# First piece behind two residual norms taken in five chunks as separate products on the residual and on the unscaled new term

## What is computed

```
x = x + rms_norm(mixed, mix_post_g)      # mixed = (gates ...) @ w_out
h = rms_norm(x, ffn_pre_g)
gt, up = split(h @ w_gate_up)            # 2 x 2816 columns
f = (silu(gt) * up) @ w_down
x = x + rms_norm(f, ffn_post_g)
h = rms_norm(x, norm1_g_2)               # second block
z = h @ w_in_2                           # lru_x first (1024 columns)
```

## Time and profile before

| what | value |
|---|---|
| median of three runs | 909.71 us |
| the profiled execution | 910.08 us, of which 908.0 us are the span of instructions |
| TensorE, VectorE, ScalarE, GpSimd busy | 99%, 81%, 64%, 4% of the span |
| granted TensorE clock | 0.999 in the mean, 9 (90% or more) in each of 40 slices |
| HBM traffic | 177 GB/s over the span |
| chain that ended last | TensorE 66%, issue 24%, VectorE 6%, ScalarE 2% |

### The profile page before, as it was taken

The page is one execution under the profiler, slowest core; times in us unless marked ns, Lnnn a source line. Parts: engine busy times, 40 slices in busy tenths (PEclk is TensorE's granted clock), DMA queues, the critical chain, the costliest instruction groups (busy, mean ns, idle before and its releaser), DMA issues.

```text
span 908.0 us, 18312 instructions
## 1 busy us (share of the span) xinstructions
PE 899.3 (99%) x6623; PEld 847.7 (93%) x6623; DVE 736.6 (81%) x1361; ACT 580.8 (64%) x998; POOL 38.0 (4%) x50
## 2 busy tenths in 40 slices
PE   9999999999999999999999999999999999999997
PEld 7999999999999999998888888999999999999886
DVE  5999898888989988689888646889979988888533
ACT  5649878797877575566666535679656755666332
POOL 1000111111110000000000000100000000000000
PEclk9999999999999999999999999999999999999999
DMA  9577588877875647456555555445447455555601
GB/s 335 181 267 231 143 199 236 248 219 218 241 203 192 209 166 247 145 161 236 196 186 185 193 187 170 147 171 189 143 134 257 158 192 185 182 179 175 228 1 47
DMA packets 48510, 172.04 MB, mean 189 GB/s; under 512 B 5668, under 2 KB 6344, under 8 KB 48328
## 3 DMA queue, kind: packets, MB, share of 16 engines
q1 hardware_dynamic: 43488, 154.74, 51.2%
q0 software_dynamic: 2880, 10.49, 6.1%
q10 hardware_dynamic: 2088, 6.08, 1.8%
HBM read 159.72 MB, written 1.09 MB: 177 GB/s over the span
## 4 chain that ended last, share of the span: by engine, by line
PE 66%; issue 24%; DVE 6%; ACT 2%; DMA 1%; POOL 1%; SPq 0%; POOLq 0%; ACTq 0%; DVEq 0%
PE A L472 10%; PE A L473 10%; PE A L474 10%; PE B L696 5%; PE A L504 4%; PE B L504 3%; PE B L472 2%; PE B L473 2%; PE B L474 2%; PE A L506 2%; DVE w_lo L1397 2%; PE B L506 2%; PE B L777 2%; PE A L777 1%; PE A L485 1%
## 5 line engine op out<-in xcount | busy, mean ns | idle before, releaser
L1397 DVE TENSOR_TENSOR w_lo<-raw,w_hi 128x1024 fp32r<-128x1024 f32 x249 | 301.8, 1220 | 72.7 <-ACT w_hi L930 72.1
L930 ACT ACTIVATE w_hi<-raw 128x1024 fp32r<-128x1024 f32 x249 | 259.4, 1051 | 74.6 <-PE A L778 20.9
L472 PE MATMUL A<-h,w_hi 128*128 128x256 f32 x952 | 274.5, 288 | 0.2 <-DVE sc L2017 0.2
L474 PE MATMUL A<-h,w_lo 128*128 128x256 f32 x952 | 269.2, 283 | 0.0
L473 PE MATMUL A<-h,w_hi 128*128 128x256 f32 x952 | 269.2, 283 | 0.0
L472 PEld LDWEIGHTS A<-h,w_hi 128*128 128x128 f32 x952 | 182.1, 191 | 3.3 <-issue 2.6
L473 PEld LDWEIGHTS A<-h,w_hi 128*128 128x128 f32 x952 | 182.3, 191 | 0.3
L474 PEld LDWEIGHTS A<-h,w_lo 128*128 128x128 f32 x952 | 182.2, 191 | 0.0
L472 PE MATMUL B<-h,w_hi 128*128 128x256 f32 x352 | 100.1, 284 | 0.0
L473 PE MATMUL B<-h,w_hi 128*128 128x256 f32 x352 | 99.6, 283 | 0.0
L474 PE MATMUL B<-h,w_lo 128*128 128x256 f32 x352 | 99.6, 283 | 0.0
(11 more groups left out here) (313 smaller groups left out, 1635.0 us busy)
## 6 DMA issues: line engine op xcount, KB each, us to landing
raw<-in_weights_dram SPq DMA_DIRECT2D x289, 512.0 KB, 4.3
w_lo<-raw POOLq DMA_DIRECT2D x20, 512.0 KB, 4.8
csrow<-cs_dram ACTq DMA_DIRECT2D x9, 512.0 KB, 4.9
x<-in_x_dram SPq DMA_DIRECT2D x4, 256.0 KB, 5.3
bd<-in_lru_w_dram ACTq DMA_DIRECT2D x1, 1024.0 KB, 5.7
out_dram<-m_wide SPq DMA_DIRECT2D x3, 256.0 KB, 2.1
raw<-in_weights_dram SPq DMA_DIRECT2D x2, 256.0 KB, 4.8
par<-in_params_dram SPq DMA_DIRECT2D x1, 379.0 KB, 6.3
```

The source lines that it names most:

```text
L472: mm(dst, wh, lo, start=first, stop=False, skip_group_check=free)
L474: return mm(dst, wl, hi, start=False, stop=last, skip_group_check=free)
L930: F(w_hi[:, s, :], raw[:, s, :], ACT.Copy).then_inc(hi_ready, 1)
L1397: V.tensor_tensor(w_lo[:, s, :], raw[:, s, :], w_hi[:, s, :].bitcast(F32), ALU.subtract).then_inc(lo_ready, 1)
```

## The change

For five chunks (1 to 5) of the first piece behind each norm the product of the weights with `g*(x + m*s*gm)` is taken in two parts: one on `g*x` with the old residual, and one on `g*gm*m` with the new term before its scale `s`. The second goes to a bank of its own, VectorE multiplies it by `s` and adds it to the output of the first piece. TensorE takes two chunks of the first part, then the sums, then three more chunks, the spread, and then the five chunks of the second part (`apart_residual`); the dummy products go, and in `scaled_four` the first piece leaves out these chunks. ScalarE makes ten high parts for each norm (`x_part`, `m_part`), VectorE ten low parts. For the first norm they are made between the pieces of the preceding stage. For the second norm, the parts on `x` are made by ScalarE at the beginning of the down projection and by VectorE between `split_rest_lo(0)` and `lru_rates`, the parts on `m` with the output chunks. VectorE copies the scale and multiplies the second product (`m_products_scaled`) between `residual_scaled` and `sum_squares`. The diff, with context cut:

```diff
@@ -82,6 +82,7 @@
 DOWN1_REST = KF - 2 * KD
+APART = (1, 2, 3, 4, 5)
@@ -184,10 +185,14 @@
         zero = sb("zero", [P, P], F32R)
+        gains = sb("gains", [P, 2, KD])
         mean = sb("mean", [P, T])
...
         scale = sb("scale", [P, TT])
+        s0a = ExitStack()
+        m_stage = sb("m_stage", [P, 2 * T], F32R, s0a)
+        s0a.close()
         stage = sb("stage", [P, 2, T])
@@ -235,6 +240,8 @@
+
+        m_apart = sb("m_apart", [P, len(APART) - 2, 2 * T], F32R, s4)
         s4.close()
@@ -313,6 +320,12 @@
+
+        mix_x = {k: hid[:, KD + k, :] for k in APART}
+        mix_m = {k: hid[:, 2 * KD + k, :] for k in APART}
+        down_x = {k: h[:, k, :] for k in APART}
+        down_m = {k: m_apart[:, i - 2, :] if i > 1 else m_stage[:, :] if i else hid[:, KF, :] for i, k in enumerate(APART)}
+        mix_apart, down_apart = B[:, 0, 0:T], B[:, 3, 0:T]
@@ -368,6 +381,9 @@
         last_scale = sem("last_scale")
+        gains_ready, x_high, x_low, m_high, m_low = (
+            sem("gains_ready"), sem("x_high"), sem("x_low"), sem("m_high"), sem("m_low"))
+        m_products, m_scaled, apart_added = sem("m_products"), sem("m_scaled"), sem("apart_added")
@@ -541,6 +557,21 @@
+            def apart_residual(p, n, bank, evacuated, summed_n, norm_n, squares_n, norm_bank, xs, ms, apart):
+
+                pe.wait_ge(lo_ready, split_order(p))
+                pe.wait_ge(x_low, n * len(APART))
+                pe.wait_ge(m_copied, evacuated)
+                for i, k in enumerate(APART):
+                    if i == 2:
+                        residual_sums(summed_n, squares_n, norm_bank)
+                    tile(p % RING, k, xs[k][:, T:], xs[k][:, 0:T], bank, i == 0, False, True)
+                spread_scale(norm_n, norm_bank)
+                pe.wait_ge(m_low, n * len(APART))
+                for k in APART:
+                    ins = tile(p % RING, k, ms[k][:, T:], ms[k][:, 0:T], apart, k == APART[0], k == APART[-1], True)
+                ins.then_inc(m_products, 1)
+
@@ -548,12 +579,15 @@
                     pe.wait_ge(stage_hi, operand + k + 1)
-                    for j in range(4):
-                        mm(banks[j], w_hi[:, (p + j) % RING, at], h_hi[:, k, :], start=k == 0, stop=False)
-                        mm(banks[j], w_lo[:, (p + j) % RING, at], h_hi[:, k, :], start=False, stop=False)
+                    for j in range(k in APART, 4):
+                        mm(banks[j], w_hi[:, (p + j) % RING, at], h_hi[:, k, :], start=k == 0 and j > 0, stop=False,
+                           skip_group_check=True)
+                        mm(banks[j], w_lo[:, (p + j) % RING, at], h_hi[:, k, :], start=False, stop=False,
+                           skip_group_check=True)
                     pe.wait_ge(operand_ready, operand + k + 1)
-                    for j in range(4):
-                        ins = mm(banks[j], w_hi[:, (p + j) % RING, at], h_lo[:, k, :], start=False, stop=k == KD - 1)
+                    for j in range(k in APART, 4):
+                        ins = mm(banks[j], w_hi[:, (p + j) % RING, at], h_lo[:, k, :], start=False, stop=k == KD - 1,
+                                 skip_group_check=True)
                         if k == KD - 1:
@@ -750,7 +784,7 @@
                 chunk_piece(MIX0 + m, 0, ring_bank(72 + m), h_hi, h_lo)
-            spread_residual(3, 11, 2 * KD, B[:, 0, :], norm_bank=B[:, 3, :])
+            apart_residual(UP1, 1, UP1_BANKS[0], KD - 1, 3, 11, 2 * KD, B[:, 3, :], mix_x, mix_m, mix_apart)
@@ -805,7 +839,7 @@
                     ins.then_inc(output_done, 1)
-            spread_residual(5, 13, 4 * KD, B[:, 2, :], norm_bank=B[:, 1, :])
+            apart_residual(LRUX0, 2, LRU_BANKS[0], KD + 5, 5, 13, 4 * KD, B[:, 1, :], down_x, down_m, down_apart)
@@ -1171,10 +1205,24 @@
+            def x_part(k, gain, parts):
+
+                F(parts[k][:, T:], x[:, k, :], ACT.Identity, scale=col(gain, k)).then_inc(x_high, 1)
+
+            def m_part(k, n, parts):
+
+                act.wait_ge(gains_ready, n + 1)
+                act.wait_ge(m_copied, n * KD + k + 1)
+                F(parts[k][:, T:], m_wide[:, k, :], ACT.Identity, scale=gains[:, n, k:k + 1]).then_inc(m_high, 1)
+
...
                 split_hi(MIX0 + m + LEAD)
+                if m < len(APART):
+                    x_part(APART[m], "ffn_pre_g", mix_x)
                 act.wait_ge(pieces_done, MIX0 + m + 1)
                 copy_and_square(A[(72 + m) % 3][:, 0:T], m_wide[:, m, :], sq_wide[:, m, 0:T])
+                if m in APART:
+                    m_part(m, 0, mix_m)
@@ -1236,6 +1284,10 @@
             F(sp[:, 1, :], sp[:, 0, :], ACT.Exp, scale=-1.0).then_inc(sp_exp, 1)
+            act.wait_ge(pieces_done, DOWN1)
+            for k in APART:
+                x_part(k, "norm1_g_2", down_x)
+
@@ -1255,6 +1307,8 @@
                     F(sq_wide[:, m, 0:T], m_wide[:, m, :], ACT.Square).then_inc(squares_ready, 1)
+                    if m in APART:
+                        m_part(m, 1, down_m)
@@ -1810,6 +1864,33 @@
+            def x_part_low(k, i, n, gain, parts):
+
+                dve.wait_ge(x_high, n * len(APART) + i + 1)
+                V.scalar_tensor_tensor(parts[k][:, 0:T], x[:, k, :], col(gain, k), parts[k][:, T:].bitcast(F32),
+                                       ALU.mult, ALU.subtract).then_inc(x_low, 1)
+
+            def m_part_low(k, n, parts):
+
+                dve.wait_ge(m_high, n * len(APART) + APART.index(k) + 1)
+                V.scalar_tensor_tensor(parts[k][:, 0:T], m_wide[:, k, :], gains[:, n, k:k + 1],
+                                       parts[k][:, T:].bitcast(F32), ALU.mult, ALU.subtract).then_inc(m_low, 1)
+
+            def m_products_scaled(n, dst, rstd, apart):
+
+                dve.wait_ge(m_products, n)
+                after(own.up(V.tensor_copy(dst, rstd)))
+                V.tensor_tensor(dst, apart, dst, ALU.mult).then_inc(m_scaled, 1)
+
+            def add_apart(n, dst, bank):
+
+                dve.wait_ge(m_scaled, n)
+                V.tensor_tensor(dst, bank, dst, ALU.add).then_inc(apart_added, 1)
+                dve.wait_ge(apart_added, n)
+
+            V.tensor_tensor(gains[:, 0, :], col("mix_post_g", 0, KD), col("ffn_pre_g", 0, KD), ALU.mult).then_inc(gains_ready, 1)
+            V.tensor_tensor(gains[:, 1, :], col("ffn_post_g", 0, KD), col("norm1_g_2", 0, KD), ALU.mult).then_inc(gains_ready, 1)
+
@@ -1846,9 +1927,14 @@
                     add_square(sq_wide, 2 * KD, c)
+                if c < len(APART):
+                    x_part_low(APART[c], c, 0, "ffn_pre_g", mix_x)
                 if c == KD - 2:
                     add_next_to_last(sq_wide, 2 * KD)
+                if c - 1 in APART:
+                    m_part_low(c - 1, 0, mix_m)
             residual_scaled(12, 11, "mix_post_g", "ffn_pre_g", hi_n, 0, up1_sums, up1_rstd)
+            m_products_scaled(1, stage3[:, 0, :], up1_rstd, mix_apart)
             sum_squares(sq_wide, 3 * KD)
@@ -1874,7 +1960,9 @@
                 dve.wait_ge(staged, pair + (STAGED_FFN1 - 1))
-                V.tensor_tensor(stage2[:, b, :], banks[0], rs, ALU.mult).then_inc(scaled, 1)
+                if pair == 0:
+                    add_apart(1, stage3[:, 0, :], banks[0])
+                V.tensor_tensor(stage2[:, b, :], stage3[:, 0, :] if pair == 0 else banks[0], rs, ALU.mult).then_inc(scaled, 1)
                 split_lo(p + UP_LEAD, turn)
@@ -1928,6 +2016,8 @@
             split_rest_lo(0)
+            for i, k in enumerate(APART):
+                x_part_low(k, i, 1, "norm1_g_2", down_x)
             lru_rates()
@@ -1936,8 +2026,11 @@
                     split_rest_lo(c)
+                if c - 1 in APART:
+                    m_part_low(c - 1, 1, down_m)
             add_next_to_last(sq_wide, 4 * KD)
             residual_scaled(14, 13, "ffn_post_g", "norm1_g_2", hi_n, KD, down_sums, down_rstd)
+            m_products_scaled(2, sc_sum[:, :], down_rstd, down_apart)
             sum_squares(sq_wide, 5 * KD)
@@ -1955,7 +2048,10 @@
                     dve.wait_ge(xp_ready, c - 1)
-                V.tensor_tensor(u2[:, c % 2, LRU_K - 1:], LRU_BANKS[c], rs, ALU.mult).then_inc(copied, 1)
+                if c == 0:
+                    add_apart(2, sc_sum[:, :], LRU_BANKS[0])
+                V.tensor_tensor(u2[:, c % 2, LRU_K - 1:], LRU_BANKS[c] if c else sc_sum[:, :], rs,
+                                ALU.mult).then_inc(copied, 1)
```

## The result

The changed kernel takes **915.0 us** (median of 6 runs, 913.46 to 915.88) against 909.89 us of the kernel before (6 runs, 909.65 to 910.31): 1.0053 times as long, 95% interval 1.0043 to 1.0063. It is slower, as forecast, by 5.1 us where 3.9 were forecast. The profiled execution took 915.52 us, its span 913.4.

A forecast was written before the change was run, and what follows sets the result against it. TensorE, busy 99% of the span, was taken to bound the kernel, with VectorE lacking slack before the second norm. 0.11 (first norm) plus 3.76 (second) gave 3.87 us, so 913.6 us; 8-in-10 range 911.5 to 916.0.

The forecast's parts named there:

- First norm: At the first norm TensorE's 1.25 us gain turns into a wait for VectorE's second additions; TensorE goes on 0.11 us later.
- Copy and multiplication: On VectorE ahead of the second additions after each norm: together 0.66 to 0.90 us, taken as 0.78.
- Second norm, VectorE: VectorE's last addition of squares before the second norm ends at 571.37 against 567.17, 4.20 us late; bounds 2.2 to 6.0.
- The 1.95 for the parts on x: Before the second norm, VectorE's five parts on x, 0.39 us each, move the first addition of halves by 1.95 us.
- The 1.95 for the parts on m: Before the second norm, VectorE's parts on m make up 1.95 us of the 4.20 us lag.
- the 0.30 for ScalarE's turns: Before the second norm, VectorE waits 0.30 us longer for ScalarE, net of idle time used up.
- rival a: Clock falls in TensorE's 3.6 us hole before the second norm's sums; loss grows by 1.5 to 3.5 us; chance 0.12.
- nothing gives time back: Behind the second norm, TensorE has next to no idle time (0.2 us) that could give back the 3.76 us delay.
- The extra addition ahead of VectorE's first multiplication: In the stage after a norm, this 0.45 us addition delays nothing that TensorE waits for.
- The untouched stretches: Stretches of the kernel that the change does not touch: forecast difference 0.
- The clear win (b): At both norms parts fit VectorE's idle time and square sums are on time: 2.6 us gained, 907.1; chance 0.07.
- The absorbed lag (c): VectorE's lag is absorbed but second additions bind, 0.11 at first norm, about 0 at second: 909.8; chance 0.07.
- The late first norm (d): First norm also late as one ScalarE turn slips past a piece: 0.4 to 0.8 us more, 914.4; with forecast 0.74.

The follow-up runs named there:

- experiment 3: Changed kernel with VectorE's parts on x and the lambda steps ahead of the second norm's early splits: 909.85 us; parts on x alone moved: 911.89 us.
- experiment 2: Changed kernel plus sixteen dummy products on zeros ahead of the second norm's sums: 913.01 us, ratio 1.0037 to the kernel before.
- the early order: Changed kernel with VectorE's parts on x and the small lambda steps both put ahead of the second norm's early splits: 909.85 us, ratio 1.000.
- experiment 6: Kernel before plus an unused 64-byte buffer, with the dummy products of the spread left out: 912.72 us, ratio 1.0031.
- experiment 5: Fifth piece moved ahead of later sums: early-order kernel, both norms 909.8 us, first norm 908.37; change at first norm alone 906.88; buffer-only kernel 908.55.

## Why the prediction was right, and where it was off

**First norm (+0.11 forecast).** Right within 0.13: -0.02 in the changed kernel, -0.01 alone. The mechanism too: nothing late before the sums, TensorE's gain turned into a wait for VectorE's second additions, 1.17 us where about 1.36 follow from the forecast (391.30 - 389.94). The first sum moved by 1.30 us (376.54 against 375.24), of which 0.60 is the later start of the whole run: 0.70 where 0.72 was forecast; the second group by 1.03 - 0.60 = 0.43 where it was 0.55. Copy and multiplication cost 0.45 and 0.34, together 0.79; I had taken 0.78. The later scale held nothing up there.

**Second norm, VectorE (4.20 late).** Right: the last addition ends 4.43 us later (571.60 against 567.17), and 0.20 of that is already there at the last early split, 551.63 against 551.43, before any part is made. The 1.95 for the parts on x is borne out by experiment 3: taking them away shortens the hole from 3.84 to 1.87 us, by 1.97. The 1.95 for the parts on m and the 0.30 for ScalarE's turns are right as a sum only; no run parts them. Without the clock the stretch measured 4.00 over before (experiment 2), forecast 3.76.

**Second norm, the clock (rival a, 0.12).** This is the step that failed. I wrote "the hole is hardly longer than the one in the tail", where the clock had fallen after 3.55 us, and gave the fall little chance. It fell 2.2 us into a wait of 3.84, and cost 1.9 us. One fall in the tail was taken for a threshold. It was one sample of a wide scatter: from TensorE's last product to the fall it is 1.8 us in the tail of the kernel with the parts on x early, 3.1 in the changed kernel's and 4.4 in the early order's, and experiments 3 and 6 show falls with waits of 1.87 and 1.66 us. The 1.9 lies inside the 1.5 to 3.5 that the rival had priced, but by another path, which is luck: I had TensorE end after VectorE, while in the trace it still waits 0.94 us for VectorE at the later sums, and the cost is the slow sums and the nine products ahead of the spread (experiment 3). A product took 0.21 us at the lower clock, not 0.24. The better reading was in the earlier trace rows: the engine is kept busy with dummies in gaps of 1 to 2 us, and without them these gaps cost 3.8 us at the two norms (experiment 6), so a gap of 3.6 would hardly be free. The Trainium skill, "TensorE: Matmul & The Clock Gate", Part 1 (the HAM clock gate), says that sustained work must come before the clock is full again. The traces agree: the return came 5.2 us after work had resumed in the changed kernel, 5.6 and 3.0 us at the two norms of the kernel without dummies. That bears on the price of a fall, not on its chance, which is where the forecast went wrong.

**Behind the second norm ("nothing gives time back").** Off by +0.74 to the first scan, +0.77 in the early order. I had costed the later second additions at their wait alone. Two terms can be read. The spread comes 4.02 us behind the later sums instead of 3.32, 0.70 more, of which TensorE waits 0.42 (the timeline above), since two splits and the moment now stand between the late additions and GpSimd's power. The extra addition ahead of VectorE's first multiplication, put at 0, takes 0.46. That multiplication so comes 5.42 us behind the later sums instead of 4.21, and at the first scan 0.74 of these 1.21 us are left. How the two terms share the 0.74 wasn't tried. That the stretch follows VectorE fits TensorE's wait of 2.04 us in experiment 5.

**The untouched stretches (0).** They came out 1.78 us shorter and hid a quarter of what the second norm and the stage behind it lost (5.90 + 0.74). The forecast had no term for the placement of buffers, and could hardly have had its size: nothing in one trace shows it. From the 3.87 of the forecast, +2.14 at the second norm, -0.13 at the first, +0.74 behind, -1.78 elsewhere and +0.60 at the start of the run lead to the 5.44 between the spans. The sum came out near the truth partly by luck, since a missed loss and a missed gain cancelled.

**The other rivals.** The clear win (b) needed the square sums to be in time at both norms: they were late by 4.2 at the second, and even with them in time (experiment 3) the kernel isn't faster, since the gain is waited away at the later sums. The absorbed lag (c) didn't happen, though 909.85 is what the early order gives: its condition, that VectorE end its additions before 567.8, is just what that order fulfils. The late first norm (d) didn't happen either: that norm came out 0.02 us shorter.

## What to carry to other kernels

Taking work off TensorE's path by giving a vector engine more of it pays only where that engine has slack in the very stretch ahead of the wait, and only if TensorE has independent work to fill what is waited for next: here the first norm had the slack, and the gain appeared (1.4 to 1.8 us) when one piece was moved ahead of the next sums. Before parts are added to an engine that runs turn by turn with another, look for its last long wait and put them there, not behind it. And compare a change that declares new buffers with the old kernel plus the same buffers: here that alone was worth 1.3 us.

## What the hardware did that I had not expected

- The clock falls on far shorter waits than the tail of the kernel before suggested: with TensorE waiting 1.87 us and then at work for over 2 us before the fall, and with waits of 1.02 and 1.66 us close together. Two holes of the same length, 3.84 and 3.86 us, saw it fall 2.2 us in and 0.7 us after the end. Once fallen it stayed down for 3.4 us (571.9 to 575.3, and 572.8 to 576.3) or for 6.8 us (570.0 to 576.9).
- A fall costs different amounts: 1.9 us in the changed kernel, 1.3 with the second norm alone and 0.1 with the parts on x early, depending on how much of the slow work stood ahead of the spread; and 2.4 and 1.3 us at the two norms of the kernel without dummies, where it stayed down for 6.8 and 3.4 us.
- An unused buffer of 64 bytes a partition made the down projections 0.7 and 1.0 us shorter, and the kernel 1.3 us faster than its 909.82 (ratio 0.9985).
